# Scores of the feed-forward's attention steps: the low part of q against the high part of k on half of the array's rows

## What is computed

```
def probs(q, k):
    s = jnp.einsum('bqhd,bkhd->bhqk', q.astype(jnp.float32), k.astype(jnp.float32)) * scale
    return jax.nn.softmax(jnp.where(mask, s, NEG_INF), axis=-1)

w = probs(q1, k1) - lam * probs(q2, k2)
return jnp.einsum('bhqk,bkhe->bqhe', w, v.astype(jnp.float32))
```

## Time and profile before

| | us |
|---|---|
| median of 3 runs | 3117.53 |
| lowest and highest | 3115.47 and 3119.28 |
| profiled execution, span | 3117.8 |
| PE busy | 2956.7 |
| DVE busy | 1790.1 |
| ACT busy | 1359.8 |
| scores (line 2905), PE busy | 155.8 |

### The profile page before, as it was taken

One profiled execution on the slowest core, in us unless ns is written; L12 is line 12 of the kernel. 1 busy time (PEld: TensorE's weight loads), 2 busy tenths in 40 slices (PEclk: granted clock), 3 DMA queues, 4 the chain that ended last, 5 costly groups with the idle time before them and its releaser, 6 DMA issues.

```text
span 3117.8 us, 38463 instructions
## 1 busy us (share of the span) xinstructions
PE 2956.7 (95%) x14384; PEld 2402.1 (77%) x14384; DVE 1790.1 (57%) x2858; ACT 1359.8 (44%) x2499; POOL 231.0 (7%) x314
## 2 busy tenths in 40 slices
PE   7999999768999999999999999999999999999997
PEld 6778787557678777777888778788788777787875
DVE  6767746357426666566566665655666555334454
ACT  5654625344224444454444444544444443222233
POOL 0201100110000110001011000011110000000000
PEclk9999989879999999999999999999999999999998
DMA  5536432837654443544443435535342244232221
GB/s 178 187 131 231 134 129 78 237 120 221 194 151 112 115 115 115 176 134 122 124 115 107 117 95 171 157 101 149 88 119 81 92 159 132 84 95 86 80 77 53
DMA packets 377576, 402.59 MB, mean 129 GB/s; under 512 B 25641, under 2 KB 277845, under 8 KB 377392
## 3 DMA queue, kind: packets, MB, share of 16 engines
q1 hardware_dynamic: 360624, 341.32, 37.1%
q0 software_dynamic: 16768, 58.81, 5.3%
HBM read 341.19 MB, written 58.91 MB: 128 GB/s over the span
## 4 chain that ended last, share of the span: by engine, by line
PE 56%; DVE 13%; ACT 5%; issue 3%; POOL 1%; DMA 0%; SPq 0%; ACTq 0%; DVEq 0%; POOLq 0%
PE c_bank L2613 45%; PE b_S L2905 3%; PE b_O L2931 2%; DVE c_w L2292 2%; DVE b_m L2499 2%; PE b_S L2622 1%; ACT b_p L2219 1%; PE b_WT L2917 1%; PE b_O L2622 1%; DVE c_rows L2303 1%; ACT c_junk L2062 1%; DVE b_p L2492 1%; DVE c_rows L2310 1%; PE b_S L2885 1%; DVE b_wT L2517 1%
## 5 line engine op out<-in xcount | busy, mean ns | idle before, releaser
L2613 PE MATMUL c_bank<-c_hT,c_w 128*128 128x512 f32 (+1 forms) x4416 | 1026.8, 386 | 15.3 <-DVE c_hT L2330 15.3
L2613 PEld LDWEIGHTS c_bank<-c_hT,c_w 128*128 128x128 f32 x4416 | 796.9, 190 | 171.0 <-issue 18.2
L2613 PE MATMUL c_bank<-c_w,c_fT 128*128 128x512 f32 x2112 | 508.6, 393 | 0.0
L2292 DVE TENSOR_TENSOR c_w<-c_raw,c_w 128x1024 fp32r<-128x1024 f32 x334 | 405.0, 1220 | 166.1 <-ACT c_w L2041 164.8
L2041 ACT ACTIVATE c_w<-c_raw 128x1024 fp32r<-128x1024 f32 x334 | 351.8, 1057 | 258.3 <-PE c_bank L2613 225.9
L2613 PEld LDWEIGHTS c_bank<-c_w,c_fT 128*128 128x128 f32 x2112 | 390.5, 188 | 86.5 <-issue 3.4
L2219 ACT ACTIVATE b_p<-b_S,b_nm 128x512 f32<-128x512 f32 (+3 forms) x288 | 180.3, 631 | 592.6 <-DVE b_nm L2500 592.6
L898 PE MATMUL a_bank<-a_w,a_hT 128*128 128x512 f32 (+1 forms) x1224 | 300.2, 401 | 0.0
L2613 PE MATMUL c_bank<-c_w,c_hT 128*128 128x512 f32 x1152 | 276.2, 396 | 7.8 <-DVE c_w L2292 4.0
L898 PEld LDWEIGHTS a_bank<-a_w,a_hT 128*128 128x128 f32 (+1 forms) x1224 | 220.7, 183 | 61.2 <-issue 3.8
L2613 PEld LDWEIGHTS c_bank<-c_w,c_hT 128*128 128x128 f32 x1152 | 218.5, 191 | 55.7 <-DVE c_w L2292 5.3
(11 more groups left out here) (363 smaller groups left out, 3306.2 us busy)
## 6 DMA issues: line engine op xcount, KB each, us to landing
c_raw<-in_ffn_w_gate SPq DMA_DIRECT2D x88, 512.0 KB, 4.9
c_raw<-in_ffn_w_up SPq DMA_DIRECT2D x88, 512.0 KB, 4.2
c_raw<-in_ffn_w_down SPq DMA_DIRECT2D x88, 512.0 KB, 4.2
a_raw<-in_w_in SPq DMA_DIRECT2D x40, 1024.0 KB, 5.2
b_k<-split_kT SPq DMA_DIRECT2D x72, 256.0 KB, 4.9
b_v<-split_v SPq DMA_DIRECT2D x36, 512.0 KB, 3.6
c_raw<-in_w_out SPq DMA_DIRECT2D x32, 512.0 KB, 5.2
c_raw<-in_ple_w_gate SPq DMA_DIRECT2D x32, 512.0 KB, 4.3
```

What stands on the lines that cost most here:

```text
L2292: V.tensor_tensor(w[:, e[1] % SLOTS, 1], raw[:, n % RAW], w[:, e[1] % SLOTS, 0].bitcast(F32), ALU.subtract).then_inc(split_ready, 1)
L2613: ins = T.matmul(out, lhs(k, a), rhs(k, b), start=first and k == 0 and n == 0, stop=end and k == blocks - 1 and n == 2)
```

## The change

The two matmuls of q's low part no longer take all 128 rows. Each now takes 64 rows, those on which the high part of k lies, and so computes low by high alone; the product of the two low parts is not computed any more. For the two to stand on different halves of the array, component 1 of `kk` is stored the other way round: its high part on partitions 64 to 127, its low part on 0 to 63. `load_k` therefore makes four transfers of 128 KB for a block in place of two of 256 KB, and `k_in` counts to 64. The order within a step is new too: first, for each component, the matmul of q's high part (128 rows) and the mask where there is one; then the two half matmuls, one after the other, component 0 on rows 0 to 63, component 1 on rows 64 to 127, into the two banks of `b_S`. The last of them raises `s_done`.

```diff
@@ load_k
-                for a in range(2):
-                    sp.dma_start(kk[a * HD:a * HD + HD, n % 4].bitcast(F32),
-                                 split["kT"][h, a, :, :, kc * 512:kc * 512 + 512].rearrange("c d t -> d c t")).then_inc(k_in[n % 4], 16)
+                for a in range(2):
+                    for c in range(2):
+                        at_ = (a ^ c) * HD
+                        sp.dma_start(kk[at_:at_ + HD, n % 4, c].bitcast(F32),
+                                     split["kT"][h, a, c, :, kc * 512:kc * 512 + 512]).then_inc(k_in[n % 4], 16)
@@ block.tensor
-                        pe.wait_ge(k_in[c % 4], 32 * (c // 4 + 1))
+                        pe.wait_ge(k_in[c % 4], 64 * (c // 4 + 1))
...
                     for z in range(2):
-                        for a in range(2):
-                            ins = T.matmul(S[:, z, 0:cols], qq[:, x % 4, a, z], kk[:, c % 4, z, 0:cols], start=a == 0, stop=a == 1 and kc < g)
+                        T.matmul(S[:, z, 0:cols], qq[:, x % 4, 0, z], kk[:, c % 4, z, 0:cols], start=True, stop=False)
                         if kc == g:
-                            ins = T.matmul(S[:, z, cols - P:cols], ident_r[:], mask[:], start=False, stop=True)
+                            T.matmul(S[:, z, cols - P:cols], ident_r[:], mask[:], start=False, stop=False)
+                    for z in range(2):
+                        half = slice(z * HD, z * HD + HD)
+                        ins = T.matmul(S[:, z, 0:cols], qq[half, x % 4, 1, z], kk[half, c % 4, z, 0:cols], start=False, stop=True)
                     ins.then_inc(s_done, 1)
```

## The result

The changed kernel is slower: 3131.74 us in the median (3129.38 to 3133.52, four runs) against 3116.5 us of the kernel before beside it, a ratio of 1.0047 with a 95% interval of 1.0033 to 1.0061. A second measurement gave 1.0048 (1.0034 to 1.0062). That is some 15 us, between 10 and 19. The profiled execution spans 3131.8 us from its first instruction to its last; the time of that run is 3133.52 us, so a run's time stands 1.7 us above its span.

A forecast was written before the change was run, and what follows sets the result against it. The prediction took PE to bound the attention steps. To 3117.8 us it added 31 for the large and small steps together (middle of 23 to 39) and took off 5 hidden in waits: 3144 us, range 3112 to 3168.

The forecast's parts named there:

- drain and overlap: Forecast case for the half matmuls: PE drains at each shape change, the two stream side by side; 3144 us, chance 0.57.
- What bounds the kernel: Attention steps, 900 to 2500 us: PE sets the pace, busy 1548.4 of 1600 us; its step cost counts nearly one for one.
- Two changes of shape: Around the half matmuls: load waits 0.32 us, bare load 0.11, then 0.32 and 0.11; 0.86 us against 0.69 before.
- what I had named as a sign: In the trace after, a full step would take 1.16 to 1.27 us in place of 0.99.
- The overlap: In the low-part pair, the second half matmul streams beside the first, starting at most 0.11 us after it.
- The second load: Weights of the second half matmul: up to 0.11 us later if loads go in series, +0.28 instead of +0.17 us.
- What hides some of it: PE's waits for split and combined probabilities shrink in the attention steps: at most 9 us hidden, 5 taken.
- The key loads: SP's key issues, 72 becoming 144 of half size at 0.3 to 0.6 us each: priced at nothing.
- serial pair: Rival: the second half matmul streams after the first, +0.40 us a large step; 3167 us, chance 0.14.
- no drain: Rival: fp32r shape changes drain nothing and the pair runs side by side; faster, 3091 to 3103 us, chance 0.17.
- unchanged: Rival: neither drain nor overlap, so the two half matmuls cost what they cost before; 3118 us, chance 0.08.
- a late SP: Rival: SP's longer key issues delay the transfers queued behind them, the forecast plus 11 us; 3155 us, chance 0.04.

The follow-up runs named there:

- same rows: The changed kernel with both half matmuls on rows 0 to 63, so that they cannot stream together: 3153.65 us, ratio 1.0112.
- the transfers alone: The kernel before with only the changed key transfers (four of 128 KB), its four full score matmuls kept: 3114.94 us, ratio 0.9993.

## Why the prediction was right, and what in it was off

The prediction was 3144 us, slower, in a range of 3112 to 3168; the time is 3131.74. The likeliest case, drain and overlap, is the one that happened. By its own steps:

**What bounds the kernel** held in its direction: what PE gains or loses in the steps moves the time, and nothing else that was tried does. "Nearly one for one" did not hold: of work added to PE 65 to 85 per cent came out in the stretch, of work taken away just under half.

**Two changes of shape** held, with the numbers of the plain fp32 rows carried over to fp32r: 0.33 us from the last 128-row matmul to the load (I had 0.32), 0.44 from the pair's start to the full array's load (0.11 + 0.32), 0.34 to the second matmul (0.34). The Trainium skill's "TensorEngine Tiling (Array Packing)", Key Properties, has the drain at a change of mode; the trace agrees now for fp32r too, with those 0.33 us. A full step takes 1.05 us to the item's first matmul, and 1.16 with the 0.11 lost behind it, the low end of what I had named as a sign.

**The overlap** held: same rows cost 0.22 us more a step. The Trainium skill's "TensorE: Matmul & The Clock Gate", Part 3, has tiles on other rows start some 4 ns apart; the trace agrees, the starts in the pair differ by less than 0.01 us.

**The second load** is the term that was mis-sized. I took the middle between a load beside the first one and a load behind it, for want of a row. The traces show it beside: +0.17 us a full step, the low end, and 24.5 us over all steps where I had 31; the low end of my sum was 23, the case that the prediction priced at 3136 us. On the same rows it does come 0.11 us later, which is what the upper end had assumed. That 24.5 and 23 lie so close is in part luck: the steps of 128, 256 and 384 keys cost 0.18, 0.23 and 0.16 us more, where the low end was 0.13 (with 128 keys the load came 0.20 us behind the mask, and I had 0.15), and the diagonal steps of 512 keys only 0.12, where I had 0.17.

**What hides some of it** was off by little: I took 5 us of at most 9. From 24.5 us of PE's work 18.3 come out in the stretch of the steps, so some 6 are hidden there, and the runs put the whole at some 15, with an interval of 10 to 19. The waits named do become shorter, by 5.8 us together. The two errors go the same way: 31 - 5 = 26 was expected, 24.5 - 6 = 18.5, near the 18.3, is seen in the stretch. The 6 may be more: by the clock records of the traces, TensorE was granted the 1.2 GHz level for 13.7 us of this stretch before and for 23.9 us after, which alone can cost up to 5 us; then up to 11 are hidden. Over all runs these times lie between 10.2 and 27.3 us, and whether the change has a part in them is not shown. The profiled span is only 14 us longer, mainly because its first step starts 5 us earlier (916.3 against 921.4); across all traces this start lies between 911.8 and 921.4 us, ahead of every matmul that was edited.

**The key loads** were rightly priced at nothing. An issue takes as long as one of twice the size, the dear end of what I had allowed, and the transfers alone do not slow the kernel.

**The rivals**: serial pair, refuted by the same-rows run, which is that rival built; no drain, refuted by the holes; unchanged, by the result; a late SP, by the transfers alone.

## What to carry to other kernels

Here a pair of half-row matmuls saved one matmul's stream, but standing alone between full-row matmuls it paid two drains and two bare loads: 0.40 us against 0.23 us saved in a full step, and a loss at every size of block in these runs (128 to 512 keys). Group such work, so that more than two pairs of 512 columns share one change to half rows and back (at two, the runs show no difference), or leave it on the full array, and look in the trace of before for any change of shape, even of another type, to price it. Of time saved on the bounding engine, ask what the next waits give back: here it was half.

## What the runs showed that I had not expected

A wait of PE can cost more than its own length. In the kernel without the low part, PE waits 2.4 us for the combined probabilities before 1005.9 us. Three stretches around this (start:end, length, busy PE, PEld, DVE, ACT, POOL with counts, granted clock, DMA):

```profile
1000.00:1003.30 3.30, 3.30 (x19) 2.67 (x17) 0.26 (x1) 2.94 (x4) 0.60 (x1) 1.00 0.25 66
1003.30:1005.90 2.60, 0.19 (x1) 0.00 (x0) 2.56 (x5) 0.58 (x1) 0.00 (x0) 1.00 0.32 118
1006.00:1010.40 4.40, 4.40 (x13) 3.47 (x14) 2.87 (x12) 2.74 (x8) 0.11 (x1) 0.61 0.36 119
```

And PE in order of time there:

```profile
1005.91 0.33 PE L2918 MATMUL b_WT<-ident,b_p 128*128 128x128 f32 x1 [2.41 <-DVE b_p L2494]
1005.99 4.59 PE L2615 MATMUL c_bank<-c_hT,c_w 128*128 128x512 f32 x12
1010.42 0.28 PE L2932 MATMUL b_O<-b_v,b_wT 128*128 128x256 f32 x1
```

PE works through the first stretch, is nearly idle through the second, and in the third the granted clock is 0.61 on the mean, so mostly the 1.2 GHz level. Twelve matmuls take from 1005.99 to 1010.42 there, 4.43 us, where the twelve of the earlier trace rows take 2.74. Some 1.7 us went on top of the wait.

Not every such wait is followed by this. In the kernel before PE waits 2.18 us at the same place of its schedule, and the clock stays at 1.00:

```profile
1013.60:1015.80 2.20, 0.10 (x1) 0.00 (x0) 2.17 (x5) 0.26 (x1) 0.00 (x0) 1.00 0.23 69
1016.00:1018.80 2.80, 2.80 (x13) 2.31 (x14) 1.41 (x6) 2.14 (x8) 0.00 (x0) 1.00 0.60 186
```

Nor does it explain why a saving of 60 us gave only 30: by the clock records the 1.2 GHz level covers 10.2 us of the stretch of the steps without the low part, and 13.7 us before.

Two loads of weights into different rows of the array go out at the same time (0.19 us for two of 0.18), and so the pair pays one bare load, not two; into the same rows the second comes 0.11 us later.
